# mLSTM in a 1-core Trainium2 kernel: denominators and mean squares computed as rows, the root on ScalarE and the reciprocal on rows, in place of a product with a scaled diagonal

## The reference

```python
S = einsum(q, k) * exp(D - m_t)                # decayed scores, causal
num = inter * (q C_in) + S v                   # 256 values a token
den = inter * (q . n_in) + S.sum(-1)           # one number a token
h = num / maximum(abs(den), exp(-m_t))
hm = rms_norm_2(h, out_norm_g)                 # mean over the 256 values of a head, EPS 1e-6
ym = hm * sigmoid(mo) * silu(mgate)
```

## Time and profile before

| | before |
|---|---|
| median of 3 runs | 1464.46 us (1463.51 to 1465.22) |
| the profiled execution | 1464.48 us |
| its span, first to last instruction | 1462.7 us |
| instructions | 27764 |
| busy: PE, PEld, DVE, ACT, POOL | 99%, 91%, 75%, 56%, 19% of the span |
| HBM traffic | 239.03 MB, mean 163 GB/s |

### The profile page before, as it was taken

One profiled execution on the slowest core, in us unless ns is written; L12 is line 12 of the kernel. 1 busy time (PEld: TensorE's weight loads), 2 busy tenths in 40 slices (PEclk: granted clock), 3 DMA queues, 4 the chain that ended last, 5 costly groups with the idle time before them and its releaser, 6 DMA issues.

```text
span 1462.7 us, 27764 instructions
## 1 busy us (share of the span) xinstructions
PE 1442.1 (99%) x9821; PEld 1332.3 (91%) x9821; DVE 1100.1 (75%) x2183; ACT 822.1 (56%) x1492; POOL 283.6 (19%) x348
## 2 busy tenths in 40 slices
PE   8999999899999999999999999999999999999998
PEld 7888899888888888889988888999999999999998
DVE  6777679977766777667777776888769769976983
ACT  6666448566544656445466654556745455576442
POOL 1111113311102111024221112422240125121000
PEclk9999999999999999999999999999999999999999
DMA  6657754556555666555456656543343555434443
GB/s 210 199 187 217 230 169 139 168 184 196 182 189 181 195 188 191 184 190 173 144 185 189 196 163 188 160 129 107 97 116 116 172 141 150 124 94 121 125 134 112
DMA packets 245558, 239.03 MB, mean 163 GB/s; under 512 B 15193, under 2 KB 244425, under 8 KB 245465
## 3 DMA queue, kind: packets, MB, share of 16 engines
q1 hardware_dynamic: 244888, 236.73, 52.8%
q10 hardware_dynamic: 576, 1.05, 0.2%
HBM read 236.70 MB, written 1.05 MB: 163 GB/s over the span
## 4 chain that ended last, share of the span: by engine, by line
PE 90%; DVE 6%; ACT 2%; issue 1%; DMA 1%; POOL 1%; ACTq 0%; DVEq 0%; POOLq 0%
PE bank L614 80%; DVE w_lo L1700 2%; PE bank L971 1%; PE bank L927 1%; PE bank L909 1%; ACT w_hi L1060 1%; PE bank L838 1%; PE bank L848 1%; PE bank L892 1%; PE bank L977 1%; PE bank L987 1%; DMA work<-in_x_dram 1%; PE bank L908 0%; PE bank L928 0%; PE bank L957 0%
## 5 line engine op out<-in xcount | busy, mean ns | idle before, releaser
L614 PE MATMUL bank<-x_both,w_hi 128*128 128x512 f32 (+2 forms) x3552 | 805.4, 332 | 1.5 <-DVE h L1789 1.3
L1700 DVE TENSOR_TENSOR w_lo<-raw,w_hi 128x1024 fp32r<-128x1024 f32 (+1 forms) x456 | 551.5, 1233 | 214.7 <-ACT w_hi L1060 213.7
L1060 ACT CAST w_hi<-raw 128x1024 fp32r<-128x1024 f32 (+1 forms) x456 | 456.9, 1029 | 137.7 <-PE bank L614 125.0
L614 PEld LDWEIGHTS bank<-x_both,w_hi 128*128 128x128 f32 x3552 | 514.7, 189 | 4.7 <-DVE w_lo L1700 1.6
L614 PE MATMUL bank<-x_both,w_lo 128*128 128x256 f32 (+1 forms) x2480 | 496.9, 281 | 0.0
L614 PEld LDWEIGHTS bank<-x_both,w_lo 128*128 128x128 f32 x2480 | 432.4, 189 | 62.6
L614 PE MATMUL bank<-y_both,w_hi 128*128 128x512 f32 (+2 forms) x1472 | 345.7, 337 | 4.9 <-issue 3.5
L614 PEld LDWEIGHTS bank<-y_both,w_lo 128*128 128x128 f32 x1088 | 191.7, 188 | 31.3
L614 PEld LDWEIGHTS bank<-y_both,w_hi 128*128 128x128 f32 x1472 | 212.9, 189 | 5.6 <-issue 3.8
L614 PE MATMUL bank<-y_both,w_lo 128*128 128x256 f32 (+1 forms) x1088 | 215.8, 280 | 0.0
L1585 POOL TENSOR_TENSOR work<-work,rstd 128x256 f32<-128x256 f32 x88 | 63.4, 743 | 416.3 <-ACT work L1107 416.3
(11 more groups left out here) (307 smaller groups left out, 1242.4 us busy)
## 6 DMA issues: line engine op xcount, KB each, us to landing
raw<-in_ffn_w_in_dram SPq DMA_DIRECT2D x176, 512.0 KB, 3.8
raw<-in_w_in_dram SPq DMA_DIRECT2D x100, 512.0 KB, 3.6
raw<-in_ffn_w_out_dram SPq DMA_DIRECT2D x64, 512.0 KB, 4.5
raw<-in_w_out_dram SPq DMA_DIRECT2D x32, 512.0 KB, 4.2
raw<-in_ffn_w_out_dram SPq DMA_DIRECT2D x32, 384.0 KB, 3.3
raw<-in_rec_w_in_dram SPq DMA_DIRECT2D x16, 512.0 KB, 4.3
raw<-in_sg_w_in_dram SPq DMA_DIRECT2D x16, 512.0 KB, 4.4
raw<-in_rec_w_out_dram SPq DMA_DIRECT2D x8, 512.0 KB, 3.4
```

The lines of the kernel that those rows point to most:

```text
L614: i_ = mm(accs[m][:, cols], w[:, s, j, m * P:(m + 1) * P], moving, start=begin and g == 0, stop=final)
L1060: nc.scalar.copy(w_hi[:, s, 0:n, :], raw[:, s, 0:n, :]).then_inc(hi_made, 1)
L1700: TT(w_lo[:, s, 0:n, :], raw[:, s, 0:n, :], w_hi[:, s, 0:n, :].bitcast(fp32), SUB).then_inc(lo_made, 1)
```

## The change

Everything that was done with tokens on the partitions is now done on 272-wide rows that are equal on all partitions. In stage 1 PE multiplies m_pt with a full 128x128 of ones (three products, bank 4), and broadcasts a row of exp(-2m), which is now kept in g_row, into bank 5. ACT takes a third Square, of the denominators, into d_max, and DVE the maximum of that and the row. In stage 2 PE multiplies the squares with ones (two products of 272 columns, bank 5), DVE adds 256 * EPS * d_max, and ACT loads the table of the root (root_table). ACT takes the root behind the split of weights of the next unit (head_root); DVE takes its reciprocal, which is s_b: for heads 0 to 2 behind stage 0 of the next head, for head 3 ahead of its own taken. PE and ACT have no stage 3 any more. Only one of the two gate rows is transposed in kx.

```diff
@@ PE, kx
-                        for w, r in enumerate((3, 5)):
+                        for w, r in enumerate((3,)):
@@ PE, ml
                             pe.wait_ge(ms_read, n)
-                            if hd >= 2:
-                                pe.wait_ge(m_sb, n - 1)
...
-                        for j, (ja, jb) in enumerate(LT):
-                            for t, (a, b) in enumerate(LT[:j + 1]):
-                                at = MOFF[t] + ja - a
-                                pj = m_pt[:, at:at + jb - ja] if j < 2 else wide_pt(at)
-                                i_ = mm(bank[4][0:max(jb - ja, FULL), 400 + j:401 + j], pj, ones[:, 0:1], start=t == 0,
-                                        stop=t == j)
-                        i_.then_inc(m_num, 1)
+                        for t, (a, b) in enumerate(LT):
+                            mm(bank[4][:, a:L], ones[:, :], m_pt[:, MOFF[t]:MOFF[t] + L - a], start=t == 0, stop=t == 2)
+                        mm(bank[5][:, 0:L], ident[:, hd:hd + 1].broadcast_to((P, P)), g_row[:, 5, :], start=True,
+                           stop=True).then_inc(m_num, 1)
@@ PE, stage 2
-                        for j, (a, b) in enumerate(LT):
-                            for w in range(2):
-                                o = max(b - a, FULL)
-                                i_ = mm(bank[4][0:o, 408 + j:409 + j], pt[:, w, a:a + o], ones[:, 0:1], start=w == 0,
-                                        stop=w == 1)
+                        for w in range(2):
+                            i_ = mm(bank[5][:, 0:L], ones[:, :], n_sq[:, w, :], start=w == 0, stop=w == 1)
                         i_.then_inc(m_ms, 1)
-                    if stage == 3:
-
-                        pe.wait_ge(m_diag, n + 1)
-                        if hd < M_H - 1:
-                            pe.wait_ge(m_exp_new, n + 2)
-                        for j, (a, b) in enumerate(LT):
-                            sum_of = ones[:, :] if j < 2 else tri[:, TAIL - 1:TAIL].broadcast_to((P, P))
-                            i_ = mm(bank[4][:, a:b], sum_of, diag[:, j, 0:b - a], start=True, stop=True)
-                        i_.then_inc(m_bb, 1)
@@ ACT, ml
-                    if stage == 3:
-                        act.wait_ge(m_bb, n + 1)
+                        activation(d_max, bank[4][:, 0:L], ACT.Square).then_inc(m_dsq, 1)
+                    if stage == 2:
+
+                        root_table()
+                        roots_due.append(n)
+
+                roots_due = []
+
+                def head_root():
+
+                    while roots_due:
+                        n = roots_due.pop()
+                        act.wait_ge(ms_read, n + 1)
                         if n:
-                            act.wait_ge(m_taken, n)
-                        nc.scalar.copy(s_b, bank[4][:, 0:L]).then_inc(m_sb, 1)
+                            act.wait_ge(m_sb, n)
+                        activation(d_root, d_max, ACT.Sqrt, scale=1.0 / 16).then_inc(m_root, 1)
@@ ACT, each unit, behind its split_w
+                            head_root()
@@ DVE, ml_later
                         dve.wait_ge(m_num, n + 1)
-                        for r, c in small:
-                            i_ = TS(den_s[r, 0, c], bank[4][r, 400 + c.start:400 + c.stop], -1.0, None, MUL)
...
+                        dve.wait_ge(m_dsq, n + 1)
+                        TT(d_max, d_max, bank[5][:, 0:L], MAX).then_inc(m_den, 1)
+                    if stage == 2:
+
+                        dve.wait_ge(m_ms, n + 1)
                         dve.wait_ge(m_den, n + 1)
...
-                        rsqrt(den_s[:, 5, 0:3], den_s[:, 2, 0:3], den_s[:, 4, 0:3])
...
-                            i_ = TS(diag[0:b - a, j, 0:b - a], ident[0:b - a, 0:b - a], den_s[0:b - a, 5, j:j + 1], 0.25,
-                                    MUL, MUL)
-                        i_.then_inc(m_diag, 1)
+                        STT(out=d_max, in0=d_max, scalar=256 * EPS, in1=bank[5][:, 0:L], op0=MUL, op1=ADD).then_inc(ms_read, 1)
...
+                def inverse_root(n):
+
+                    dve.wait_ge(m_root, n + 1)
+                    V.reciprocal(s_b, d_root).then_inc(m_sb, 1)
+
                 def taken(hd, stage):
                     n = M_H * l + hd
                     if stage == 3:
+                        if hd == M_H - 1:
+                            inverse_root(n)
                         dve.wait_ge(m_sb, n + 1)
@@ DVE, the unit of a stage 0
                                 kind, n = steps[0]
                                 do[kind](n)
+                                if n[0]:
+                                    inverse_root(M_H * l + n[0] - 1)
                                 later = [steps[0]]
                                 steps = steps[1:]
```

More of the change, by code:

```diff
@@ L318, in build_stack @@
         g_row = region(6)
-        g_tok = region(3, 8)
-        den_s = region(8, 4)
+        g_tok = region(3, 4)
         s_b = work[:, own_at:own_at + L]
-        diag = work[:, own_at + L:own_at + L + 3 * P].rearrange("p (c n) -> p c n", n=P)
+        d_max, d_root = (work[:, own_at + k * L:own_at + (k + 1) * L] for k in (1, 2))
         k_up = cos_g
@@ L413, in build_stack @@
         m_num, m_sq, m_den, m_ms, ms_read = sem("m_num"), sem("m_sq"), sem("m_den"), sem("m_ms"), sem("ms_read")
-        m_diag, m_bb, m_sb, m_hm, m_taken = sem("m_diag"), sem("m_bb"), sem("m_sb"), sem("m_hm"), sem("m_taken")
+        m_dsq, m_root, m_sb, m_hm, m_taken = sem("m_dsq"), sem("m_root"), sem("m_sb"), sem("m_hm"), sem("m_taken")
         gate_act, ot_tr, stored = sem("gate_act"), sem("ot_tr"), sem("stored")
@@ L1495, in _ @@
                                     act.wait_ge(g_cm, l + 1)
-                                    activation(g_row[0:4, 5, :], g_row[0:4, 5, :], ACT.Exp, scale=-1.0).then_inc(g_exp, 1)
+                                    activation(g_row[0:4, 5, :], g_row[0:4, 5, :], ACT.Exp, scale=-2.0).then_inc(g_exp, 1)
                                 if ph == "mqk":
@@ L1622, in _ @@
             nc.gpsimd.memset(r_t, 0.0)
-            nc.gpsimd.memset(g_row[:, 4, :], 0.0)
+            nc.gpsimd.memset(g_row[:, 4:6, :], 0.0)
             nc.gpsimd.memset(pt[:, :, :], 0.0)
@@ L2138, in kx @@
                     V.memset(k_att[0:DH, :], 0.0)
-                    V.tensor_copy(g_tok[:, 0:2, :], bank[5][:, 3 * P:3 * P + 16].rearrange("p (t n) -> p t n", n=8))
-                    V.tensor_copy(g_tok[0:TAIL, 2, :], bank[5][0:TAIL, 3 * P + 16:3 * P + 24]).then_inc(kx_read, 1)
+                    V.tensor_copy(g_tok[:, 0:2, :], bank[5][:, 3 * P:3 * P + 16].rearrange("p (t n) -> p t n", n=8)[:, :, 0:4])
+                    V.tensor_copy(g_tok[0:TAIL, 2, :], bank[5][0:TAIL, 3 * P + 16:3 * P + 20]).then_inc(kx_read, 1)
                 def att(v):
@@ L2218, in ml_later @@
                     n = M_H * l + hd
-                    small = ((slice(0, P), slice(0, 2)), (slice(0, TAIL), slice(2, 3)))
                     if stage == 0:
@@ L2232, in ml_later @@
                         dve.wait_ge(m_num, n + 1)
[L2233 to L2241 removed]
+                        dve.wait_ge(m_dsq, n + 1)
+                        TT(d_max, d_max, bank[5][:, 0:L], MAX).then_inc(m_den, 1)
                     if stage == 2:
                         dve.wait_ge(m_ms, n + 1)
[L2245 to L2257 removed]
+                        dve.wait_ge(m_den, n + 1)
+                        STT(out=d_max, in0=d_max, scalar=256 * EPS, in1=bank[5][:, 0:L], op0=MUL, op1=ADD).then_inc(ms_read, 1)
                     if stage == 3:
```

16 lines of the change are left out of this document (removed).

## The result

| | before | after |
|---|---|---|
| median | 1463.95 us (1463.39 to 1465.22, 5 runs) | 1471.96 us (1469.99 to 1473.59, 5 runs) |
| ratio | | 1.0052 [1.0041, 1.0063] |
| the profiled execution, its span | 1464.48, 1462.7 | 1472.98, 1471.2 |

The change makes the kernel slower by 0.5%, 8.0 us by these medians. The forecast was 1471.3 us.

What follows compares the result with a forecast made beforehand. PE was taken to bound the kernel (busy 1442.1 of 1462.7 us). New waits +10.3, restarts +0.6 and PE's gain -4.1 gave +6.8 on 1464.5: 1471.3 us, range 1468.0 to 1474.3.

Steps and rivals of the forecast that it cites:

- What bounds the kernel, and the slack: PE bounds, without waits in the head; DVE's release of banks 6 and 7 has slack 0.93 us (layer 0), 0.63 (layer 1).
- DVE's part: Savings ahead of DVE's idle time only lengthen it; the reciprocal in the stretch without gaps delays what follows by 1.77 us.
- The new wait: PE at stage 1 of heads 1 to 3 waits 1.56 us in layer 0, 1.86 in layer 1: 10.3, plus 0.6 for restarts.
- PE's own work: Per head 2.86 us of PE products removed, 2.39 added: gain 0.47, 3.8 over eight heads, 4.1 with the transposes.
- the 0.3 of the small transposes: Three small transposes go from kx in each layer, six in all: 0.3 us less on PE, bounds 0 and 0.5.
- the two surcharges: Slower PE starts behind 16-column products: m_pt set 0.93 instead of 0.89, exp(-2m) row 0.54 instead of 0.46; without them gain 0.64.
- the upper end of 7.6: Upper end of the forecast's change in us: waits and restarts of 10.9 with PE's gain at only 3.3.
- ACT's part: Two table changes per head, 2.6 us, fit ACT's idle time; the root is hidden by 0.7 us ahead of the reciprocal.
- The sum: Whole kernel: +10.3 + 0.6 - 4.1 = +6.8 us, from 1464.5 to 1471.3; ends +4.7 and +7.6.
- rival 3: A second wait joins: late root ahead of DVE's reciprocal, or late maximum or projection splits; +3 us, 1474.3; chance 0.09.
- Rival 1: No wait appears at PE's stage 1, only PE's gain is left: 1460.4 us, faster; chance 0.05.
- rival 2: The reciprocal delays by half, 0.9 us, as another DVE wait absorbs the rest: +1.6, 1466.1, no change; chance 0.07.

Runs made afterwards that it cites:

- before_plus_inverse: The kernel before plus one idle 128x272 reciprocal into a spare tile on DVE, behind stage 0 of heads 1 to 3, 6 in all; 1471.18 us, 1.0047.
- cheap_inverse: The changed kernel with DVE's 8 reciprocals of 128x272 replaced by copies, semaphores kept; 1462.21 us, 0.9988.
- both_early_no_tables: The changed kernel with root, reciprocal and taken moved ahead, and without the mLSTM's table changes, scale wrong; 1458.88 us, 0.9962.
- no_tables: The changed kernel without its 16 table changes in the mLSTM, the root made a Square (scale wrong); 1469.40 us, 1.0035.
- both_early: The changed kernel with ACT's root ahead of its split, DVE's reciprocal ahead of the mask, taken ahead of a split; 1463.47 us, 0.9997.
- reordered: The changed kernel with DVE's reciprocal, taken, gating and m_pt before splits, squares' sums in bank 4, root ahead of ACT's split, head 3 earlier; 1464.42 us, 1.0001.
- after_again: The changed kernel unaltered, run again in a later round and on another chip than four other kernels; 1470.25 us, 1.0044.
- taken_first: The changed kernel with DVE's taken ahead of the gating and the split of weights in its unit; 1465.16 us, 1.0009.
- reordered_end: As reordered, but head 3's reciprocal behind the gating of the unit before the last, taken behind the scaling of the last tiles; 1459.64 us, 0.9970.
- filled_wait: The changed kernel with six unread products of ones on PE ahead of its stage 1 wait for m_taken, heads 1 to 3; 1469.27 us, 1.0035.

## Why the prediction was right

**What bounds the kernel, and the slack.** Right. PE had no wait in the head, and the slacks of 0.93 and 0.63 us decided. before_plus_inverse, which adds only the reciprocal, turned them into brackets of 0.75 and 1.06.

**DVE's part.** Right in each step. The operations taken out only lengthened the idle time ahead of the mask (3.03 us; "some 3" was said). The reciprocal moved what follows by 1.76 (1.77 was said). It is the term that carries the loss, as cheap_inverse shows.

**The new wait.** Right in place and size: 1.59 from start to start in layer 0 and 1.86 in layer 1 (7.59 where two units take 5.73), forecast 1.56 and 1.86. The brackets themselves show 1.43 and 1.72. Two small errors offset each other in it: taken ends 8.81 us behind L950 in layer 0 (1092.99 - 1084.18) where 8.88 was forecast, and L968 starts 0.14 behind that end where 0.05 was. I had named brackets of about 1.6 and 1.9, and mixed up the two: a bracket is measured from the modelled end of the last product, and so 0.15 shorter than what the wait costs. The restart cost 0.08 a time (0.1 forecast). Together 10.9 us, as forecast: by the distances 19.20 and 18.70 against the 17.53 and 16.75 of both_early_no_tables, three times each.

**PE's own work.** The step that was mis-sized. I had added 2.39 us a head: 0.93, 0.54 and 0.92. In after the three take 0.93 (1095.91 - 1094.98), 0.34 (1096.25 - 1095.91) and 0.71 (1100.17 - 1099.46): 1.98. The surcharge that I put on the row of exp(-2m), for standing behind a 16-column product, does come:

```profile
L972 PE MATMUL bank<-work,con x16: 392/476/801, 1076.7 to 1408.5; 128*128 128x272 f32 x16
```

Each row is two passes; their median is 476 ns, the least 392, so the first passes are the long ones, and the two take 0.70 where those of L950 take 0.62. What I had wrong is the end of a set. I let L613 start only when the last pass had had its full 0.23, for the row and for the squares alike. It starts 0.34 behind the start of the row, of which the first pass takes 0.31 (0.70 less the 0.39 of the second), and 0.71 behind that of the squares, of which three passes take 0.69: 0.02 to 0.03 behind the start of the last pass both times. In return L613 behind each is slower: a unit takes 3.21 where 3.10 is usual behind the products of before, twice 0.11. So 2.20 were added, and the gain is 2.86 - 2.20 = 0.66 per head, where I had 0.47. The distances give the same without that sum: from head 0 to head 1 nothing is gained (17.53 against 17.52), and each stage 3 that is gone gains 0.67. In total 8 x 0.67 + 0.3 = 5.7 where I had 4.1 (the 0.3 of the small transposes is still the forecast's, as no run shows it alone); both_early_no_tables measured 4.9 against before, in whole medians, which also hold what varies at the start. Two sums of the forecast's bounds were wrong as well, without effect on its middle: without the two surcharges (0.04 and 0.08) the gain is 0.59 a head and not 0.64, and a gain of 3.3, from which the upper end of 7.6 came, follows from none of its terms, whose least gain is 3.8. By its own terms the ends are 5.1 and 7.1.

**ACT's part.** Right for the six waits: the root was hidden by 0.8 us in layer 0 (0.7 forecast) and by 0.4 in layer 1, and no_tables showed the same waits at L968. Wrong by 0.6 us at the end of layer 1, where I had put the tables at nothing: there a load puts back the splits ahead of the output projection, and PE waits. A load took 1.28 us and the operation behind it started 1.29 after it; of the drain that the Trainium skill ("ScalarE: Activation LUTs", What ACT_TABLE_LOAD costs) puts on top, this trace shows nothing either. That page's advice to batch activations by set (section "Table sets: the hidden batching unit") was still not idle here: in both_early the same load lay on the path, and without the loads that kernel was 4.6 us faster.

**The sum.** With the measured terms it is 10.9 - 5.7 = +5.2, and that gives 1469.1 from the median before: the lowest runs of after (1469.21, 1469.79, 1469.99). The others lie up to 4.4 us higher. In the profiled execution, from the first L950 on, after takes 9.3 us more. Of this 5.4 are the waits less PE's gain there (10.9 - 5.5); 3.3 are two stretches of half clock; 0.6 is the wait for w_lo in the output projection (bracket 0.34 at 1430.07) that goes with the tables, and which I had only as a part of rival 3. So that the forecast of 1471.3 is near the median is partly luck, as errors offset each other: a gain of PE taken 1.6 us too small on one side, and on the other the 0.6 us of the tables and a cost of 1.7 us per stretch of half clock that I had not thought of.

**The rivals.** Rival 1 (no wait) and rival 2 (half the delay) are refuted by the brackets. Rival 3 asked for a bracket ahead of the reciprocal, ended by the root: it is not in after, but it is what both_early and reordered ran into. My expectations of those two erred in one and the same point: I took DVE's idle time for room, without asking when ACT could have the root ready there. The late splits for the projection, which rival 3 names too, are in after, with 0.6 us.

## What to carry over

Work taken off an engine ahead of a point where it waits for another gains nothing; work put in behind that point costs in full as soon as the slack up to the next hand-over is used up. So before an operation is swapped for another, find on which side of the wait each of the two lies, and read the slack of the hand-over from the two timelines (here 0.63 to 0.93 us against 1.77). The same instructions in another order gained 4 us instead of losing 6 to 8, but each order that I tried first moved the wait to another place, the root or a split of weights: after each move look at what is queued behind it.

## What the runs showed of the hardware that I had not expected

**Short waits of PE can be followed by half clock.** Two of the six waits in the profiled execution of after were followed by a stretch of about 3.4 us in which the granted clock was half, 1.2 instead of 2.4 GHz. Busy times in two stretches of layer 1 (us, PE, PEld, DVE, ACT, POOL, then the granted clock, the share of DMA and GB/s), of after:

```profile
1360.00:1383.00 23.00, 20.21 (x156) 19.20 (x154) 19.65 (x41) 13.84 (x28) 0.00 (x0) 1.00 0.41 109
1383.00:1389.00 6.00, 5.35 (x24) 4.83 (x25) 5.17 (x13) 2.58 (x6) 0.00 (x0) 0.72 0.44 116
```

and of after_again, with the same wait of 1.72 at the same place:

```profile
1383.00:1389.00 6.00, 5.19 (x36) 4.91 (x37) 5.76 (x14) 4.10 (x9) 0.00 (x0) 1.00 0.44 122
```

PE's timeline of after in that stretch:

```profile
1383.65 2.37 PE L968 MATMUL bank<-work 128*128 128x272 f32 x12 [1.72 <-DVE work L2254]
1385.86 1.97 PE L971 MATMUL bank<-work,ones 128*128 128x272 f32 x6
1387.68 1.12 PE L972 MATMUL bank<-work,con 128*128 128x272 f32 x2
```

L971 takes 1.82 to the next start instead of 0.93, L972 0.66 instead of 0.34. Ahead of it PE was busy for 20.21 of 23 us. A second stretch follows the wait at 1404.02. Each cost 1.7 us (20.36 against 18.70, 76.02 against 74.35). What decides whether it comes stays open: in after_again and no_tables, with the same six waits, neither came. It is no matter of these six waits alone either. Every kernel, before too, has a wait of 2.19 or 2.20 us near 255 us, and in seven of the thirteen profiles half clock follows it (after, after_again, no_tables, cheap_inverse, before_plus_inverse, taken_first, reordered_end), in six it does not. In after_again:

```profile
250.00:260.00 10.00, 7.81 (x53) 7.63 (x52) 10.00 (x21) 6.68 (x10) 0.00 (x0) 0.83 0.39 127
```

Whether the clock makes the spread of after is not shown. In filled_wait, where the waits were filled, the clock stayed full in the stretches above and the five runs lay within 1.8 us (1468.82 to 1470.58), against 3.6 in after. But no_tables, with the six waits as they are, lay within 0.6 us (1469.13 to 1469.77), and the mean clocks of the runs do not follow their times: the run of after at 1470.16 us has 0.995, the one at 1473.59 has 0.996.

**A bracket shows less than a wait costs.** With the start-to-start distance and the slower restart, each wait cost 0.24 us more than its bracket, 1.4 us for six.
